# A two-layer block with modulated input: modulation weights laid out with features on the partitions, and a first layer that opens with four column chunks at a time

## The reference

```
mod = silu(c) @ w_mod + b_mod                  # 2048 -> 3 * 2048, float32
shift, scale, gate = split(mod, 3)
h = rms_norm(x, g_pre) * (1 + scale) + shift
proj = h @ w_in                                # eleven chunks of 512 columns, and 16 more
... windowed attention, spatial gating, gated linear attention, times silu(z)
out = y @ w_out
x = x + gate * rms_norm(out, g_post)
```

## Time and profile before

| | us |
|---|---|
| median of three executions | 2982.62 |
| lowest and highest | 2982.52, 2982.68 |
| the profiled execution | 2983.63 |
| its span, first to last instruction | 2981.8 |

### The profile page before, as it was taken

One profiled execution on the slowest core, in us unless ns is written; L12 is line 12 of the kernel. 1 busy time (PEld: TensorE's weight loads), 2 busy tenths in 40 slices (PEclk: granted clock), 3 DMA queues, 4 the chain that ended last, 5 costly groups with the idle time before them and its releaser, 6 DMA issues.

```text
span 2981.8 us, 37910 instructions
## 1 busy us (share of the span) xinstructions
PE 2835.0 (95%) x13440; PEld 2346.0 (79%) x13440; DVE 1838.4 (62%) x2049; ACT 1352.2 (45%) x1741; POOL 64.0 (2%) x86
## 2 busy tenths in 40 slices
PE   1799999899999999999999999989999999999997
PEld 1578887688887788888888888868888888888886
DVE  8888988767854655555455455565655554545565
ACT  1244554444644444444454544434445445445443
POOL 0400000000000000000000000000000000000000
PEclk9899999899999999999999999989999999999999
DMA  9787678667545555556555565645554655555664
GB/s 372 279 303 267 237 249 327 215 227 231 171 142 169 192 173 171 176 198 201 188 172 173 177 190 186 228 135 176 176 177 160 229 191 176 176 177 174 194 212 141
DMA packets 165357, 604.32 MB, mean 203 GB/s; under 512 B 19192, under 2 KB 19360, under 8 KB 163904
## 3 DMA queue, kind: packets, MB, share of 16 engines
q1 hardware_dynamic: 160336, 583.08, 58.3%
q0 software_dynamic: 4848, 18.91, 2.1%
HBM read 599.79 MB, written 2.12 MB: 202 GB/s over the span
## 4 chain that ended last, share of the span: by engine, by line
PE 66%; DVE 1%; issue 1%; DMA 0%; ACT 0%; DVEq 0%; ACTq 0%; SPq 0%
PE acc L729 61%; PE psT L656 2%; PE psS L689 1%; PE psS L679 1%; PE psT L662 1%; PE psS L696 0%; DVE x L605 0%; DMA raw<-in_w 0%; DVE x L616 0%; DVE x L609 0%; ACT whi L304 0%; DVE wlo L408 0%; DVE stage L440 0%; DVE x L580 0%; DVE x L618 0%
## 5 line engine op out<-in xcount | busy, mean ns | idle before, releaser
L408 DVE TENSOR_TENSOR wlo<-raw,whi 128x1024 fp32r<-128x1024 f32 x672 | 822.7, 1225 | 863.6 <-ACT whi L304 860.5
L304 ACT ACTIVATE whi<-raw 128x1024 fp32r<-128x1024 f32 x672 | 711.6, 1060 | 991.4 <-PE acc L729 979.0
L729 PE MATMUL acc<-whi,xhi 128*128 128x512 f32 x2304 | 637.1, 398 | 9.9 <-DVE xlo L414 9.1
L729 PE MATMUL acc<-whi,xlo 128*128 128x512 f32 x2304 | 618.7, 390 | 0.0
L729 PE MATMUL acc<-wlo,xhi 128*128 128x512 f32 x2304 | 617.6, 390 | 0.0
L729 PEld LDWEIGHTS acc<-whi,xlo 128*128 128x128 f32 x2304 | 433.7, 188 | 92.5
L729 PEld LDWEIGHTS acc<-wlo,xhi 128*128 128x128 f32 x2304 | 433.0, 188 | 91.5
L729 PEld LDWEIGHTS acc<-whi,xhi 128*128 128x128 f32 x2304 | 423.5, 189 | 90.8 <-issue 9.5
L1245 ACT ACTIVATE whi<-raw 128x1024 fp32r<-128x1024 f32 x240 | 253.2, 1058 | 380.7 <-PE acc L1972 243.8
L1430 DVE TENSOR_TENSOR wlo<-raw,whi 128x1024 fp32r<-128x1024 f32 x232 | 283.0, 1223 | 163.2 <-ACT whi L1245 162.0
L1972 PE MATMUL acc<-whi,hhi 128*128 128x512 f32 x960 | 278.3, 412 | 13.6 <-DVE hlo L1441 8.3
(11 more groups left out here) (291 smaller groups left out, 1944.1 us busy)
## 6 DMA issues: line engine op xcount, KB each, us to landing
raw<-in_w SPq DMA_DIRECT2D x912, 512.0 KB, 3.5
mraw<-in_w_mod SPq DMA_DIRECT2D x150, 512.0 KB, 4.2
scr<-in_w_mod SPq DMA_DIRECT2D x31, 512.0 KB, 6.3
b_stage<-in_w_mod SPq DMA_DIRECT2D x11, 512.0 KB, 6.2
gate_row<-in_bg POOLq DMA_DIRECT2D x16, 256.0 KB, 5.2
gb<-cum_rows POOLq DMA_DIRECT2D x2, 1536.0 KB, 8.8
x<-in_x SPq DMA_DIRECT2D x1, 2048.0 KB, 8.2
gain<-in_g_post POOLq DMA_DIRECT2D x2, 1024.0 KB, 6.5
```

The lines of the kernel that those rows point to most:

```text
L304: act.activation(whi[:, n % SLOTS, :], raw[:, n % SLOTS, :], ACT.Copy).then_inc(s_hi, 1)
L408: dve.tensor_tensor(wlo[:, n % SLOTS, :], raw[:, n % SLOTS, :], whi[:, n % SLOTS, :].bitcast(F32), ALU.subtract).then_inc(s_lo, 1)
L729: m = pe.matmul(acc[c % 2][:, tb, :], a[:, kk, tile], b[:, n % SLOTS, k * CW:(k + 1) * CW], start=(kk == 0 and q == 0), stop=(kk == GK * g ...
```

## The change

1. **Layout.** `w_mod` is stored transposed: 128 output features on the partitions, their 2048 inputs along the row. One DVE instruction multiplies such a tile by `silu(c)` (now a row, broadcast to all partitions) and sums the products into one column through its accumulator output. Layer 0's shift and scale come as 32 tiles of 128x2048 (1 MB, three buffers), in the order scale and shift of k tile 0, of k tile 1, and so on; everything else as 128 halves of 128x1024 (`mraw`, two buffers).
2. **What goes.** `macc`, its clearing, the wait of each addition for the last, and the units `ms`, `ma`, `mg` with their DVE reads. POOL makes no `wlo` any more.
3. **The start.** x is fetched first. The first 32 granules of layer 0 take four chunks at a time (`TOGETHER`), so that each pair of k tiles of h serves four granules; chunks 2 and 3 are summed in the four banks of `psS` and `psT`. x is transposed unscaled ahead of the loop, copied to SBUF, and ACT applies scale and shift (`fill_hi`), in both layers. Layer 1 opens with two chunks at a time.
4. **The late halves.** 80 of them in steps 35 to 116 of layer 0, 16 in steps 1 to 10 of layer 1 (the last columns of layer 1's shift and scale), 32 in every second step from 14. SP queues the halves of step `r` ahead of the weights of granule `r + 2`.
5. **Gate.** The gate comes as columns, is multiplied by `g_post`, written to memory by POOL, and read back broadcast into `gain`.
6. **Moved work.** Small products that were in steps 12 to 32 start at step 33; the levels start at step 42, three steps apart; window attention starts at steps 50, 58, 66, 74; the order of the z chunks differs.
7. **Products over 64 rows.** `sc` and `s` now do both halves of the rows in one go, alternating between rows 0 to 63 and 64 to 127, into two banks.

```diff
+TOGETHER = (4, 2)
 def place(l, r):
-    half = GPC // 2
-    if l == 0 and r < 2 * GPC:
-        return r // half % 2, half * (r // GPC) + r % half
-    return divmod(r, GPC)
+    n = TOGETHER[l]
+    return (r % n, r // n) if r < n * GPC else divmod(r, GPC)
...
+def late_step(i):
+    if i < 80:
+        return 0, 35 + i * 82 // 80
+    if i < 96:
+        return 1, 1 + (i - 80) * 10 // 16
+    return 1, 14 + 2 * (i - 96)
...
# SP
+        sp.dma_start(x[:], dram["x"].rearrange("(b p) n -> p b n", p=P)).then_inc(s_x, 16)
+        for n in range(3):
+            tile(n)
+        for n in range(SLOTS):
+            weights(n)
+        for j in range(GPC):
+            for n in range(4 * j + 3, min(4 * j + 7, EARLY)):
+                tile(n)
+            for n in range(4 * j + 4, 4 * j + 8):
+                weights(n)
+        for n in range(4 * GPC + 4, DEPTH * GRAN1 + 2):
+            for i in LATE_AT.get(divmod(n - 2, GRAN1), []):
+                half(i)
+            if n < DEPTH * GRAN1:
+                weights(n)
...
# ACT, fill_hi for h
+                for k in range(2):
+                    last = act.activation(src[:, cols], (bank_t(name) if l else xT_of(i))[:, cols], ACT.Identity,
+                                          scale=scale[:, l, kt:kt + 1], bias=shift[:, l, kt:kt + 1])
...
# ACT, loop
                 if l == 0 or r >= AHEAD:
                     hi(GRAN1 * l + r)
+                if l == 0 and place(l, r)[0] == TOGETHER[l] - 1 and r < TOGETHER[l] * GPC:
+                    fill_hi(("h", l, place(l, r)[1]))
...
# DVE
-            dve.scalar_tensor_tensor(out=macc_of(q)[:, cols], in0=slot, scalar=csil[:, kt:kt + 1],
-                                     in1=macc_of(q)[:, cols], op0=ALU.mult, op1=ALU.add).then_inc(s_macc, 1)
+        def tile(n):
+            dve.wait_ge(s_m[n % 3], 16 * (n // 3 + 1))
+            kt, third = n // 2, 1 - n % 2
+            dve.scalar_tensor_tensor(out=big[n % 3], in0=big[n % 3], scalar=1.0, in1=crow[:], op0=ALU.mult,
+                                     op1=ALU.mult, accum_out=mcol[:, third, kt, 0:1]).then_inc(s_macc, 1)
+        def late(i):
+            dve.wait_ge(s_m[3 + i % 2], 16 * (i // 2 + 1))
+            dve.scalar_tensor_tensor(out=mraw[:, i % 2, :], in0=mraw[:, i % 2, :], scalar=1.0,
+                                     in1=crow[:, part * MOD_W:(part + 1) * MOD_W], op0=ALU.mult, op1=ALU.mult,
+                                     accum_out=mcol[:, third, kt, part:part + 1]).then_inc(s_macc, 1)
...
# DVE, loop
+                if l == 0 and h_fill(l, r) is not None:
+                    for n in range(4 * (r // 4), 4 * (r // 4) + 4):
+                        if n >= 2:
+                            tile(n)
+                    columns_of(0, r // 4)
-                if r >= (AHEAD if l else R_HALF):
+                if l == 0 or r >= AHEAD:
                     lo(GRAN1 * l + r)
+                if l == 0 and h_fill(l, r) is not None:
+                    fill_lo(("h", l, h_fill(l, r)))
...
# PE, unit sc (unit s likewise)
+                for k, (kcol, qcol) in enumerate(spans):
+                    for half, out in enumerate((bank, pair_bank)):
+                        rows = slice(half * G_DK, (half + 1) * G_DK)
+                        m = pe.matmul(out[:, k * P:(k + 1) * P], key[rows, kcol:kcol + P], query[rows, qcol:qcol + P],
+                                      start=True, stop=True)
```

More of the change, by code:

```diff
@@ L915 @@
 UNIT1 = {name: i for i, name in enumerate(n for s in STEPS1 for n in units1(*s))}
[L917 to L937, removed]
+EARLY = 2 * KT
+LATE = [(0, 2, kt, half) for kt in range(KT) for half in range(2)]
+LATE += [(1, third, kt, half) for kt in range(KT) for third in range(2) for half in range(2)]
+LATE += [(1, 2, kt, half) for kt in range(KT) for half in range(2)]
+def late_step(i):
[4 more added lines that the diff above has]
+    return 1, 14 + 2 * (i - 96)
+LATE_AT = {}
+for i in range(len(LATE)):
+    LATE_AT.setdefault(late_step(i), []).append(i)
+SCALED = [max(i for i, m in enumerate(LATE) if m[:2] == (1, 1) and m[2] == 2 * j + 1) for j in range(GPC)]
+GATED = [max(i for i, m in enumerate(LATE) if m[:2] == (l, 2)) for l in range(DEPTH)]
 def first_block(nc, ctx, x, rings, ps, dram, ident, s_next=None):
     raw, whi, wlo = rings
-    acc, psT, psS = ps
+    acc, ps_t, ps_s = ps
+    psT = [ps_t[:, i, :] for i in range(2)]
+    psS = [ps_s[:, i, :] for i in range(2)]
     def sb(name, shape, dt=F32):
@@ L1294, in _ @@
             if l == 0:
+                for i in range(GPC):
+                    fill_copy(("x", 0, i), xT_of(i))
                 act.wait_ge(s_ang, 1)
@@ new lines, in columns_of @@
+        def columns_of(l, j):
+            kts = slice(2 * j, 2 * j + 2)
+            if l == 0:
+                dve.wait_ge(s_macc, 4 * j + 4)
+                if j == 0:
+                    dve.wait_ge(s_gpre, 48)
+            else:
+                dve.wait_ge(s_macc, EARLY + SCALED[j] + 1)
+                summed(0, kts)
+                summed(1, kts)
+            dve.tensor_tensor(shift[:, l, kts], mcol[:, 0, kts, 0], mbias[:, l, 0, kts], ALU.add)
+            link(dve.scalar_tensor_tensor(out=scale[:, l, kts], in0=mcol[:, 1, kts, 0], scalar=1.0,
+                                          in1=mbias[:, l, 1, kts], op0=ALU.add, op1=ALU.add))
+            dve.tensor_tensor(scale[:, l, kts], scale[:, l, kts], gpre[:, l, kts], ALU.mult).then_inc(s_mcol, 1)
@@ L1881, in unit @@
                 _, _, i, odd = name
[L1882 removed]
+                if odd:
+                    return
+                pair_bank = bank_s(("sc", l, i, 1))
+                need(pe, (s_sfree[(UNIT1[name] + 1) % 2], (UNIT1[name] + 1) // 2))
                 if i < 0:
```

637 lines of the change are left out of this document (283 added, 354 removed).

## The result

| | before | after |
|---|---|---|
| median, us | 2982.65 | 3032.26 |
| lowest and highest | 2982.52, 2984.9 | 3028.73, 3037.41 |
| span of the profiled execution | 2981.8 | 3031.6 |

The changed kernel is slower by 1.7%: ratio 1.0166, interval 1.0151 to 1.0181. The forecast was 2948 us. No single step explains the 84 us between them, so the trace is cut into stages first.

A forecast was written before the change was run, and what follows sets the result against it. PE was taken to bound the kernel from about 150 us on, waiting for DVE and transfers before. Terms -29 - 9.5 - 8 + 6 - 2 + 8 = -34.5 us, against the 2982.6 median, gave 2948 us; range 2908 to 2974.

The forecast's parts named there:

- DVE in the middle of layer 0: Layer 0, steps 35 to 91: DVE nearly as loaded as PE, 204 against 210 us; charged +6 us (0 to 20).
- Costed at nothing: Gate's way through memory, layer 1's halves from step 14, ACT's scale and shift there, second block: no cost.
- Two of my own signs: Forecast wrong if PE idles over 20 us in the middle, or layer 0 ends later than 515 us.
- The third: Forecast wrong if the first 32 granules end after 200 us.
- The start, -29: Opening of layer 0: first granule at 37 us, four-granule periods of 17.5 us, loss 86 instead of 115.0 us.
- the rival at 1.2 GHz: PE stays at 1.2 GHz through the opening: +26 at the start in place of -29, 3003 us; chance 4%.
- The start of layer 1, +8: Layer 1, steps 1 to 10: 16 halves share two buffers and PE waits; charged +8 us (0 to 15).
- PE work that leaves: One-column products, gate products and transposed key pairs: PE work removed or added, together -9.5 us.
- products over 64 rows: `sc` and `s` in both layers: alternating row halves partly run at once, -8 us (bounds 0 and -27).
- DVE's product with accumulator runs at half pace: Rival: tiles of 4.6 us slow the opening and DVE binds later, some 3070 us; chance 7%.

The follow-up runs named there:

- (1): Changed kernel with the decay product `dz` of levels 1 to 7 one step later: 3008.57 us.
- 8: Changed kernel with DVE multiplying only 512 of each late half's 1024 columns, the others left out of the sums: 3007.19 us.
- 10: Changed kernel with the edits of (1) and 8 together: 2991.43 us.
- (5): Changed kernel with layer 1's gated linear attention 14 steps earlier, gate product at step 19 and levels from 28: 3027.58 us.
- (15): Changed kernel with only the four buffers of kernel 13 for the 16 halves at layer 1's start: 3015.4 us.
- kernel 13: Kernel 11 with the first four halves of layer 1 issued behind the weights of granule 123: 2979.85 us, ratio 0.9992.
- (4): Changed kernel with DVE normalising x before mask, angles and the first two tiles: 3026.6 us.
- (3): Changed kernel with `sc` and `s` in the old order, all of rows 0 to 63, then 64 to 127: 3031.31 us.
- (12): Kernel 11 with the old order of the row halves: 2985.1 us, ratio 1.0011.
- Kernel 11: Changed kernel with edits (1), (4) and (5), plus four buffers instead of two, with earlier issue, for layer 1's 16 starting halves: 2983.63 us.
- 14: Kernel 13 with four halves moved from layer 0's tail into its middle: 2977.89 us, ratio 0.9981.

## Why the prediction was wrong

**The account.** Layer 0's middle, +21.6: moving `dz` one step takes 10.5 (1). The other 11 stay open. Less load on DVE shortens this middle (8, 10), but the change had added only about 4 us of DVE's work to these granules, and the overlap of the two attentions, which the earlier place took away in layer 1 (5), was not taken away in layer 0. Layer 1, restart to step 86, +38.6: four buffers, with the issue times that they allow, take 15.9 (15), the step of `dz` 14.8 (1), the earlier linear attention 4.7 (5), together 35.4. Each of these was measured by itself, and kernel 13, which has all three, has layer 1 at 319.5 against 316.9.

**The step that failed** is "DVE in the middle of layer 0", +6 us (0 to 20), and with it "Costed at nothing", where layer 1's middle should have stood and didn't. I compared sums of busy time, DVE 204 against PE 210, and found room. DVE's sum was about right (191.3 in the trace), yet it is busy only 76% of the stretch and not 97%. What I left out is the wait for a PSUM bank: `dz` stands directly behind the pair that filled both banks, and DVE begins to read them only 1.2 to 2.7 us later. The code said it beforehand: `dz` at `R_LEVEL + 3 * i` and `sc` of the level before at the same step, where in the old pace a whole step stood between them. "Three steps apart" is an item of my own account of the change, and I gave it no price. What to hold against the term is PE's idle time: it grew by 28.7 us in layer 0's middle (4.2 to 32.9), beyond the 20 that I had given as the upper end, of which 23.5 are waits of `dz` (17.5 for `st`, 6.0 for `stx`). For layer 1's middle, 24.1 us more idle and 23.9 in all, there was no term at all. Two of my own signs said so: PE idle over 20 us in the middle, and layer 0 ending after 515 (549.1). The third, a first stretch of 32 granules ending after 200, stayed quiet (189.6).

**The start, -29: measured -12.5.** PE's first granule came at 45.0 and not 37, of which 6.3 us are DVE's order (4): I had counted the two tiles ahead of the sum, but not that DVE would wait for constants until 20.32. Bursts start 18.7 us apart at first, not 17.5:

```profile
45.00 2.07 PE L1963 MATMUL acc<-whi,hhi 128*128 128x512 f32 x4 [8.38 <-DVE hlo L1464]
...
63.73 2.08 PE L1963 MATMUL acc<-whi,hhi 128*128 128x512 f32 x4 [5.83 <-DVE hlo L1464]
...
82.47 2.07 PE L1963 MATMUL acc<-whi,hhi 128*128 128x512 f32 x4 [5.00 <-DVE hlo L1464]
```

From 45.00 to the last burst at 176.93 that is 131.9 instead of 122.5 us. With the 8.0 of the first granule it makes 17.4, against the 16.5 that are missing. The form was right (bursts with gaps of 3.6 to 8.8 us, clock 0.83 from 45 to 190 us). My estimate took 408 GB/s for the queue, the rate of ten microseconds in the earlier trace rows, where the opening moves 315. Why it moves no more isn't shown: from 45 to 190 us DVE waits 24.7 us for tiles, and SP 69.8 us for DVE to free their three buffers, and no run changed either. I also priced the last burst of the rival at 1.2 GHz at 13 us instead of 21.8, so that rival should have stood near 3012 us and not 3003.

**The start of layer 1, +8: measured +14.6** in this stage, and 15.9 us of layer 1 come back when it is taken away (15). The mechanism stood in the prediction (two buffers, a turn of transfer and DVE), sized at 40 us for ten granules; they took 44 (563.4 to 607.5), and the stage lost further time behind them.

**PE work that leaves, and products over 64 rows.** From its start to the next product a full pair of `sc` takes 1.09 us instead of 1.64; the three units of a window group, 3.2 us together (1.08 and twice 1.06), are now two pairs of 0.65 and 1.06. Over 16 full pairs and 8 groups that is 9 + 12 = 21 us of PE's time, where I took 8 and bounded it by 27. The page shows only 6.9 less in all; I put the difference down to products at the lower clock (mean granted clock 0.970, before 0.987), which no kernel here measured apart. And PE waited for `psS` just there, so that the time went into the wait: the alternation undone costs nothing (3) or some 1.5 us (12). What the joining of two halves in one unit is worth on the path was not tried.
The Trainium skill (TensorEngine Tiling (Array Packing), Theoretical Speedup) gives up to 2x for two row tiles; measured is 1.5x for the full pairs of `sc` (1.64 against 1.09), and 2x for `s` with 256 columns (1.06 for one half of the rows, 1.06 for both).

**The rival "DVE's product with accumulator runs at half pace"** is out. A tile of 2048 takes 2.29 us (2.21 until the accumulator read starts) and a half of 1024 1.22, and reading the accumulator 0.08. The tiles in one of their three buffers, to 192 us, and the halves of layer 0's middle:

```profile
L1471 DVE SCALAR_TENSOR_TENSOR mraw<-mraw,crow 128x2048 f32<-128x2048 f32 x11 | 25.2, 2290 | 6.1 <-DMA mraw<-in_w_mod 6.1
L1478 DVE SCALAR_TENSOR_TENSOR mraw<-mraw,crow 128x1024 f32<-128x1024 f32 x52 | 63.5, 1222 | 6.8 <-DMA mraw<-in_w_mod 6.2
```

The Trainium skill (Vector Engine (DVE) Microarchitecture Reference, Points that are easy to get wrong) has half the throughput for this instruction with two sources in SBUF that are not bf16; the measurement shows no halving, and it decides. The change's central idea, columns by accumulating, takes DVE about as long as the sums before (a half 1.22 us and its read 0.08, a piece before 1.28). The losses that the experiments took back came from what was moved along with it. The 12% that I gave to a slower kernel stood on this rival and on a PE that stays cold, and neither was the mechanism.

## What to carry to other kernels

When a change packs small steps closer, draw for each shared bank who fills it, who wants it next, and what its reader has to finish first; then ask whether enough work stands between the filling and the next use. Here the reader came 1.2 to 2.7 us after the pair, one granule of 2.7 us covers that, and no granule was left between. A sum of busy times doesn't show it. A gap on PE can cost twice, since products behind it often run at the lower clock. A gain at one place of a kernel with full middles must be followed to the end: 12 us came at the opening and 60 were given back in three other places. The order of the work and two more buffers brought back most of it (2977.9 us): 35 in layer 1 and 7 at the opening. Layer 0's middle, 247.2 us, still stands some 18 above the kernel before by the reckoning of the table.

## What the runs showed of the hardware

Products over 64 rows into different banks and from different row halves overlap also without alternation when there are two per half: `s` with 256 columns takes 1.06 us from start to the next product for eight instructions alternated and 1.07 otherwise, while `sc` with four products per half takes 1.09 alternated and 1.64 otherwise. Why the two differ I haven't tried.

Kernel 11 varied from 2978.92 to 2986.47 us over its executions, and the kernel before from 2978.19 to 2985.69 beside it, so that differences of 2 us between kernels 11 to 14 are not established one by one.
